# A two-block transformer kernel on one core: the expert rows of units 2 to 13 in engine loops, over fixed rings of slots

## What is computed

```python
q = (xt @ wq).reshape(t, 8, 2, 128)                    # 8 heads, two halves of 128
scores = einsum('thcd,hcnd->thcn', q, sub_keys)        # 128 keys a half
sv, si = top_k(scores, 16)
cand_s = sv[:, :, 0, :, None] + sv[:, :, 1, None, :]   # 256 candidates
best_s, best_p = top_k(cand_s, 16)                     # 16 experts a head and token
gate = softmax(best_s)
act = einsum('td,thkd->thk', x, u_tab[idx])            # a dot with each expert's u row
y = einsum('thk,thkd->td', gelu(act) * gate, v_tab[idx])
```

## Time and profile before

| | |
|---|---|
| median of 3 runs | 2317.18 us (2313.78 to 2320.38) |
| profiled execution, span from its first to its last instruction | 2316.7 us |
| its own device time | not given apart from the span |
| mean granted clock of TensorE | 0.962 |
| PE busy | 2045.0 us, 88% |
| DVE busy | 1719.1 us, 74% |
| ACT busy | 845.3 us, 36% |
| POOL busy | 667.6 us, 29% |
| moved by DMA | 700.42 MB, mean 302 GB/s |
| row stages (first gather to last) | 831.7 to 1469.6 us and 1641.6 to 2280.1 us |

### The profile page before, as it was taken

How to read it: one execution, slowest core, us unless ns; L and a number is a source line. 1 busy time by engine, 2 the same in 40 slices (tenths; PEclk the granted TensorE clock), 3 DMA queues, 4 the chain that set the end, 5 groups by cost and what they waited for, 6 DMA issues and landing times. The chain is left out here.

```text
span 2316.7 us, 28383 instructions
## 1 busy us (share of the span) xinstructions
PE 2045.0 (88%) x8624; PEld 1313.5 (57%) x8624; DVE 1719.1 (74%) x4183; ACT 845.3 (36%) x2058; POOL 667.6 (29%) x627
## 2 busy tenths in 40 slices
PE   8999999999989899998778778798999987787776
PEld 6779987779979665544323233296655443333232
DVE  6757776667777577778787787575787787877875
ACT  6656655666657641212111111176312121111110
POOL 1300002200001033444444444110244445445441
PEclk9999999999999999999999998999999999999999
DMA  6255433354526569999999999765699999999996
GB/s 226 99 188 190 180 104 122 119 183 175 182 97 188 207 238 407 412 421 421 421 422 421 421 422 422 307 195 208 233 415 410 421 421 421 421 422 422 422 421 267
DMA packets 138663, 700.42 MB, mean 302 GB/s; under 512 B 14392, under 2 KB 40248, under 8 KB 66872
## 3 DMA queue, kind: packets, MB, share of 16 engines
q0 software_dynamic: 73728, 536.90, 56.1%
q1 hardware_dynamic: 64824, 162.22, 20.1%
HBM read 698.03 MB, written 1.05 MB: 302 GB/s over the span
## 5 line engine op out<-in xcount | busy, mean ns | idle before, releaser
L2111 PE MATMUL bank<-ARENA 128*128 128x512 f32 x2048 | 983.1, 628 | 203.6 <-PEq L2109 201.3
L2111 PEld LDWEIGHTS bank<-ARENA 128*128 128x128 f32 x2048 | 389.4, 199 | 776.4 <-issue 775.6
L2006 POOL DMA_INDIRECT ARENA<-in_uv_rows,ARENA x512 | 570.7, 1115 | 741.0 <-PE bank L2111 642.9
L2427 DVE CUSTOM_DVE_ANT_0 ARENA<-ARENA 128x1024 f32<-128x1024 f32 x512 | 625.2, 1221 | 208.2 <-DMA ARENA<-in_uv_rows,ARENA 200.1
L157 PE MATMUL bank<-PARTS,PARTS 128*128 128x256 f32 (+6 forms) x1488 | 469.7, 316 | 0.0
L2234 ACT ACTIVATE ARENA<-ARENA 128x1 f32<-128x1 f32 x512 | 103.3, 203 | 1003.7 <-DVE ARENA L2427 1003.3
L158 PE MATMUL bank<-PARTS,PARTS 128*128 128x256 f32 (+6 forms) x1488 | 469.4, 315 | 0.0
L156 PE MATMUL bank<-PARTS,PARTS 128*128 128x256 f32 (+3 forms) x1424 | 459.2, 322 | 6.6 <-DVE PARTS L561 2.8
L157 PEld LDWEIGHTS bank<-PARTS,PARTS 128*128 128x128 f32 (+2 forms) x1488 | 285.1, 192 | 13.6 <-issue 1.0
L158 PEld LDWEIGHTS bank<-PARTS,PARTS 128*128 128x128 f32 (+2 forms) x1488 | 284.5, 191 | 14.0
L156 PEld LDWEIGHTS bank<-PARTS,PARTS 128*128 128x128 f32 x1424 | 273.1, 192 | 24.9 <-issue 4.4
(11 more groups left out here) (275 smaller groups left out, 1930.9 us busy)
## 6 DMA issues: line engine op xcount, KB each, us to landing
ARENA<-in_w_up_tiles SPq DMA_DIRECT2D x44, 1024.0 KB, 6.3
ARENA<-in_w_down SPq DMA_DIRECT2D x44, 512.0 KB, 3.6
ARENA<-in_w_out SPq DMA_DIRECT2D x32, 512.0 KB, 4.5
ARENA<-in_wq_tiles SPq DMA_DIRECT2D x16, 1024.0 KB, 13.6
ARENA<-in_w_in SPq DMA_DIRECT2D x40, 384.0 KB, 4.0
ARENA<-in_w_in SPq DMA_DIRECT2D x24, 512.0 KB, 8.7
ARENA<-in_w_in SPq DMA_DIRECT2D x40, 256.0 KB, 3.2
ARENA<-in_uv_rows,ARENA POOLq DMA_INDIRECT x512, 22.4
```

Source lines behind the costliest of these rows:

```text
L2006: nc.gpsimd.indirect_dma_start(out=slot[slot_of[i]], out_offset=None, in_=table[:, :], in_offset=bass.IndirectOffsetOnAxis(ap=picked[:, t, ...
L2111: last = mm(row_banks[t][n][:, :], diag[i % N_DIAG], slot[slot_of[i]][:, D + n * 512:D + (n + 1) * 512], start=(c == 0), stop=(c == NPICK ...
L2427: v.tensor_tensor_reduce(u, u, xn[:, t, :], 1.0, 0.0, ALU.mult, ALU.add, dots[:, t, c:c + 1]).then_inc(S("dots_ready"), 1)
```

## The change

Slots, rings and the places of gates, numbers, dots, gelus and diagonals are fixed by the row's place in its unit, so that one body of code serves many units:

```diff
-            FEW, N_FEW = 10, 110
-            slot_of = [i % FEW if i < N_FEW else (i - N_FEW) % SLOTS for i in range(len(rows))]
+            FEW = 10
+            FIRST, LATE, LAST = 2, PH, len(units) - 1
+            mid_home = [12, 13, 2, 3, 4, 5, 0, 1, 6, 7, 8, 9, 4, 5, 0, 1]
+            late_home = [10, 11, 14, 15, 12, 13, 2, 3, 6, 7, 8, 9, 4, 5, 0, 1]
+            slot_of = [i % FEW if i < FIRST * TOPK else mid_home[i % TOPK] if i < LATE * TOPK else late_home[i % TOPK]
+                       for i in range(len(rows))]
...
+            COUNTED = FIRST * TOPK - 8
...
-            N_DIAG = 4
-            diag = [arena(diag_at + i * P, P) for i in range(N_DIAG)]
...
+            diag = [arena(diag_home[home], P) for home in slot_of]
...
-            step_after_row = {1: 2, 17: 3, 21: 4, 25: 5, 29: 6, 33: 7, 49: 8, 65: 9, 81: 10}
+            step_after_row = {1: 2, 16: 3, 19: 4, 22: 5, 25: 6, 33: 7, 49: 8, 65: 9, 81: 10}
+            TAKE_SCORES = 6
```

POOL copies a unit's sixteen numbers and issues its gathers in a loop; a counter `slot_free` that it lowers itself takes the place of `row_used` from row 24 on. In units 2 to 7 eight slots serve one row a unit and four serve two, twelve in all; from unit 8 on every row of a unit has its own, sixteen in all:

```diff
+                    def numbers_now(parity):
+                        pool.wait_ge(S("late_numbers"), 1)
+                        pool.sem_inc(S("late_numbers"), -1)
+                        nc.gpsimd.tensor_copy(picked_now[parity], picked_next)
+                        pool.drain()
+                        return picked_now[parity]
...
+                    def mid_rows(unit):
+                        now = numbers_now(unit)
+                        for r in range(TOPK):
+                            if mid_home.count(mid_home[r]) == 2:
+                                freed(1 if r - 1 in (4, 5, 6, 12, 13, 14) else 5)
+                            gather(FIRST * TOPK + r, now[:, r:r + 1])
+
+                    def late_rows(unit, entered=False):
+                        now = numbers_now(unit)
+                        for r in range(TOPK):
+                            if not entered or r >= 8:
+                                freed(1)
+                            gather(LATE * TOPK + r, now[:, r:r + 1])
...
+                    pool.wait_ge(S("row_used"), COUNTED)
+                    pool.wait_ge(S("q_filled"), step_of[1, 1] + 1)
+                    with pool.Fori(0, (LATE - FIRST) // 2):
+                        mid_rows(0)
+                        mid_rows(1)
+                    pool.wait_ge(S("q_filled"), len(steps))
+                    late_rows(0, entered=True)
+                    with pool.Fori(0, (LAST - LATE - 1) // 2):
+                        late_rows(1)
+                        late_rows(0)
+                    late_rows(1)
```

PE's loop becomes six passes over sixteen rows, and a row frees its slot on the new counter:

```diff
-                        last.then_inc(S("row_used"), 1)
+                        last.then_inc(S("slot_free") if COUNTED <= i < LAST * TOPK else S("row_used"), 1)
...
-                    looped = [(132, 10)]
+                    looped = [((LATE + 1) * TOPK, LAST - LATE - 1)]
```

```diff
+                    def unit_gelus(unit, args=True, choose=True, step=None):
+
+                        for r in range(TOPK):
+                            act.wait_ge(S("dots_ready"), unit * TOPK + (r + 1))
...
+                            if r == 9 and choose:
+                                if step:
+                                    act.wait_ge(S("sc_taken"), step + 1)
+                                nc.scalar.copy(scores_now, sc_from_one[:, unit + 1, :, :]).then_inc(S("scores_now"), 1)
...
+                    for unit in range(FIRST, LATE - 2):
+                        unit_gelus(unit, step=step_of[0, unit + 2])
+                    with act.Fori(LATE - 2, LAST - 1) as it:
+                        unit_gelus(it)
...
+                    def unit_of_rows(first, turn, choose=True, numbered=True):
...
+                        for r in range(TOPK):
+                            i = first * TOPK + r
+                            dot(i, turn * (16 * slot_of[first * TOPK:(first + 1) * TOPK].count(slot_of[i])) + loaded_by(i),
+                                dots[:, r:r + 1])
+                            if r == 0:
+                                dve.wait_ge(S("gate_exp"), turn + (first + 1))
...
+                            else:
+                                unit_diagonal(r - 1)
+                            if r == 3 and numbered:
+                                gate_args(w, gate_raw)
+                                numbers_of(w, picked_next, done="late_numbers")
+                            if r == 11 and choose:
+                                dve.wait_ge(S("scores_now"), 1)
+                                dve.sem_inc(S("scores_now"), -1)
+                                first_choice_of(w, [scores_now[:, side, :] for side in range(2)])
+                            if r == 15 and choose:
+                                best_eight_of(w)
+                                next_eight_of(w)
+                        unit_diagonal(TOPK - 1)
+                        dve.sem_inc(S("unit_gelus"), -TOPK)
...
+                    with dve.Fori(0, LATE - FIRST) as it:
+                        unit_of_rows(FIRST, it)
+                    with dve.Fori(0, LAST - LATE - 1) as it:
+                        unit_of_rows(LATE, it)
+                    unit_of_rows(LAST - 1, 0, choose=False)
+                    add_out(0)
+                    unit_of_rows(LAST, 0, choose=False, numbered=False)
```

More of the change, by code:

```diff
@@ L1274, in second_layers @@
                         + [RING_AT + s * 2 * D for s in range(4)] + [UNIT_AT + s * 2 * D for s in (2, 3)])
+            SLOTS_AT += [WQ_AT + s * 2 * D for s in range(4)]
             slot = [arena(at, 2 * D) for at in SLOTS_AT]
@@ L1726, in second_layers @@
             q_ring = [shaped(Q_AT + i * 2 * T, 2, NT, P) for i in range(2)]
-            sc = [shaped(Q_AT + 4 * T + (h + PH - 1) % PH * 4 * NKEY, 2, NT, NKEY) for h in range(PH)]
+            SC_AT = Q_AT + 4 * T
+            sc = [shaped(SC_AT + (u - 1) % len(units) * 2 * NKEY, 2, NKEY) for u in range(len(units))]
+            sc_from_one = shaped(SC_AT, len(units), 2, NKEY)
+            scores_now = shaped(WORK_AT + 1520, 2, NKEY)
             base_at, gate_sum_at = region(EXTRA_AT + NCONST2 + P, 16, len(units))
@@ L1984, in x_root, with gather, freed @@
                                                 ).then_inc(S("x_rstd"), 1)
+                    def gather(i, number):
+                        nc.gpsimd.indirect_dma_start(
+                            out=slot[slot_of[i]], out_offset=None, in_=table[:, :],
+                            in_offset=bass.IndirectOffsetOnAxis(ap=number, axis=0)
+                        ).then_inc(row_loaded[slot_of[i]], 16)
+                    def numbers_now(parity):
[4 more added lines that the diff above has]
+                        return picked_now[parity]
+                    def freed(n):
+                        pool.wait_ge(S("slot_free"), n)
+                        pool.sem_inc(S("slot_free"), -n)
                     x_root(0)
-                    for i, (t, c) in enumerate(rows):
+                    for i in range(FIRST * TOPK):
                         if i == 2:
@@ L2000, in pool @@
                             pool.wait_ge(S("picked_ready"), i // TOPK + 2)
[L2001 to L2004, removed]
+                        if row_before[i] is not None:
                             pool.wait_ge(S("row_used"), row_before[i] + 1)
[L2006 to L2010, removed]
-                            x_root(1)
+                        gather(i, picked[:, i:i + 1])
+                        if i == 15:
+                            x_root(1)
+                    def mid_rows(unit):
[21 more added lines that the diff above has]
+                    late_rows(1)
                 def pe(pe):
@@ L2261, in act @@
                     gate_exp(0)
-                    for i in range(len(rows)):
+                    for i in range(FIRST * TOPK):
                         gelu(i)
@@ L2479, in dve @@
                             numbers(1)
-                        row_dots(i)
+                        dot(i, loaded_by(i), dots[:, i:i + 1])
                         if i >= 1:
@@ L2491, in dve @@
                         u = i // TOPK + AHEAD
-                        if i % TOPK == 11 and u < len(units):
+                        if i % TOPK == 11:
                             first_choice(u)
-                        if i % TOPK == 15 and u < len(units):
+                        if i % TOPK == 15:
                             second_choice(u)
-                        if i % TOPK == 3 and AHEAD <= u - 1 < len(units):
-                            numbers(u - 1)
-                        if i == NPICK + 4:
-                            add_out(0)
-                    diagonal(len(rows) - 1)
+                        if i == TOPK + 3:
+                            numbers_of(choices[1], picked_next, done="late_numbers")
+                    diagonal(FIRST * TOPK - 1)
+                    with dve.Fori(0, LATE - FIRST) as it:
[5 more added lines that the diff above has]
+                    unit_of_rows(LAST, 0, choose=False, numbered=False)
                     add_out(NT - 1)
```

119 lines of the change are left out of this document (73 added, 46 removed).

## The result

The changed kernel takes **2459.06 us** (median of 5 runs, 2454.81 to 2464.48) where the kernel before took 2314.82 us beside it (5 runs): a ratio of 1.0616, interval [1.0602, 1.0631]. It is 144 us slower. The forecast was 2308.7 us, and its range ended at 2332.

What follows compares the result with a forecast made beforehand. Row gathers at 421 GB/s were taken as the bound, with each stage's end delayed by DVE code fetches; 2316.7 - 16.7 + 7.2 + 1.0 = 2308.2, or 2308.7 us against the median, range 2299 to 2332.

Steps and rivals of the forecast that it cites:

- Loop jumps and registers: Loops of the row units: jumps, register sums, decrements and the copies on ACT and POOL are covered by idle time, 0.
- The ring: Twelve row slots, eight serving one row a unit: late gathers cost 0 to 2 us a layer, taken as +1.0 us.
- My slower rival: DVE's loop body is not held in instruction memory, so passes fetch again: 2332 or 2355 us, chance 0.20.
- Fetches: DVE code in units 2 to 13: looping saves 8.6 fetches a layer at 0.97 us each, -16.7 us.
- Early rows: Start of each layer: PE's new query order sends row 32's gather out 4.7 us later, net 3.6 a layer, +7.2 us.
- Rival 1: DVE's loop body is not held: one fetch a pass gives 2332 us, two give 2355; chance 0.20.
- rival 2: Start of each layer costs 3.5 us more, as wq loads do not cover row 36's gap: 2315.7 us, chance 0.20.
- rival 3: Start of each layer costs nothing, as wq loads and the deeper ring take up the gap: 2300.5 us, chance 0.10.
- what would show it: Signs in the row stages: q14 packets 16 to 5 or fewer, end stretch 11.5 to about 3.5 us, row 32 later.
- that sign of a slow jump: DVE's loops: waits on "issue" of over 1 us at the head of each pass would show the forecast wrong.
- GB/s below 415 anywhere in units 2 to 7: Row transfers in units 2 to 7: a rate this low would mean that the ring of 8 binds.

Runs made afterwards that it cites:

- b_drain_28: The kernel before with one POOL drain ahead of the first gather of each of units 2 to 15, both layers: 2449.89 us, ratio 1.0572.
- a_no_drain: The changed kernel with POOL's drain behind the copy of the sixteen numbers replaced by a semaphore wait: 2304.71 us, ratio 0.9945 to the kernel before.
- b_steps: The kernel before with the change's order of early query steps and scores, POOL's old waits kept: 2321.79 us, ratio 1.0017.
- a_gate: The changed kernel without the drain, POOL's wait for 24 used rows moved ahead of each unit's third row: 2303.55 us, ratio 0.994.
- a_dve_flat2: Second run of the changed kernel without the drain and with both DVE loops written out: 2320.38 us, ratio 1.0018 to the kernel before.

## Why the prediction was wrong

**The step that failed** is the one headed "Loop jumps and registers": "So do the exchange of waits for decrements, the copy of scores on ACT, of numbers on POOL (9 of 20 us busy)", all at 0. The copy of numbers costs 0.62 us and is indeed covered. The drain behind it was not costed at all. I judged POOL's cover by its busy time, but POOL's use to the kernel is its lead: it issues gathers up to nine rows ahead of their landing (at 1265.00 in the changed kernel for a row that lands 23 us later). The drain ends that lead, and what POOL's idle time covers has no bearing on it. Its price, 28 x 5.5 = 154 us, stands where 0 stood; with it the forecast's own sum, 2308.7 + 154 = 2463, is within 4 us of the result. The 154 us come from the runs and not from before, so this agreement tests only the rest of the sum.

The bound was in reach. The ring's part says what it takes to come back from an empty queue, "some 8 us"; 28 drains at 0 to 8 us is 0 to 224, and no row of before shows a drain behind an open gather. This should have been a rival on the slower side with a good chance, and the range should have held it. My slower rival sat on a different mechanism instead.

**Fetches, -16.7 us: right.** In the form without the drain the tails shorten by 9.4 and 8.9 us, 18.3 together, and 20 + 21 packets become 9 + 9, 23 fewer where 17.2 were forecast. By this comparison a packet is 0.80 us, by the written-out loops 0.75 to 0.79, by the earlier trace rows 0.97: that the term holds within 10% is in part luck, as more packets were saved and each weighed less. In the changed kernel as it stands the saving was worth next to nothing: its tails, 1.4 and 0.4 us, are those of b_drain_28, 1.6 and 0.7, which saves no packet.

**Early rows, +7.2 us: right in kind, a quarter too small.** a_no_drain loses 3.5 and 6.1 us more than before in units 0 to 2, 9.6 together, within the bounds of 4 to 12. b_steps puts 1.3 and 2.9 on PE's order and a_gate 1.1 and 1.9 on POOL's early wait, which the forecast had folded into the order. 2.4 us stay unassigned.

**The ring, +1.0 us: nothing.** Without the drain no unit from 3 to 14 loses over 0.2 us, unit 5 included.

**Sum:** forecast -8.5 us without a drain, with misses of -1.6 on the fetches and +2.4 on the early rows that nearly cancel; between the medians of a_no_drain and before it is -12.1, and the losses account for -9.7 of it. In the two spans (-13.3) the first gather also comes 5.4 us sooner, ahead of anything the change touches.

**Rival 1 is false.** Ten jumps back a layer go with 4 packets on q14 in 520 us: both bodies were held. The Trainium skill ("Runtime: NRT & Kernel Launch", "Instruction fetch mechanics") has a taken branch out of the two-page window stop for a fetch, and advises full unrolling for it. The trace shows no such fetch for these bodies, and here unrolling was the dearer form, by 15.7 us between the medians (a_dve_flat2). **Rivals 2 and 3** were about the start. By time a_no_drain, 2304.7, lies midway between the forecast and rival 3; by the losses the start cost 9.6 us, where the forecast had 7.2, rival 2 14.2 and rival 3 nothing.

Of "what would show it", in the form without the drain: q14 in the 520 us fell from 16 to 4 and the tail from 12.2 to 2.8 us, as written, and the gather of row 32 came later: 88.6 us behind the first one, before 83.2, so 5.4 where 4.7 was said (91.3 with the drain). The last gather's dot did not come sooner after it but later: the gather starts at 2257.55 and the dot at 2291.16, 33.6 us, where it was 24.4; with sixteen slots in place of twelve POOL asks further ahead. DVE's longest wait on "issue" in a layer's loops is 0.4 us, so that sign of a slow jump is absent. "GB/s below 415 anywhere in units 2 to 7" did come in the changed kernel, but the cause named beside it, the ring of 8, was not the one: without the drain 960 to 1160, units 3 to 7, runs at 421.

## What to carry to other kernels

Before costing an instruction that waits for "all before it", list what its engine has open: POOL's drain behind open gathers waited in these runs for their landing, not for the small instruction in front of it, and its price was an empty queue, not its engine's idle time. Where a single result is needed, wait on that result's own semaphore. And when a stage is bound by transfers, look at how its last DMA engine ends: here DVE's code, fetched beside full queues, showed up there, and a loop around the long body took most of it away.

## What the runs showed that was not expected

- A drain on POOL behind open gathers ends as the last of them lands. It left POOL silent for 23.5 us at 1266.56, the queue empty for 3.6 us, and cost 5.5 us; the same copy with a semaphore let the gather out 0.9 us after its end. The Trainium skill ("VectorE: DVE Perf Modes", "The DRAIN you can't avoid") describes under that name a pipeline flush after each operation of VectorE, about the operation's length less 266 ns. That is another thing than this drain instruction on POOL, and no run here shows its figure.
- A gap in a full queue lets a late DMA engine catch up: 28 gaps took the tails from 12.2 and 10.7 us to 1.6 and 0.7 with the fetches unchanged.
- Packets that go with DVE's code lengthened the tail (16 of them 12.0 us); six that go with ACT's and POOL's did not. Whether those go through another DMA engine, whose lateness stays under that of the last one, was not looked into.
- Each kernel's profile has its own start: the first gather lay between 826.1 and 831.7 us in the profiles of one unchanged early part, so that differences of a few us between single spans say little.
